# The triangular inverses of the chunk scan: in the scan's matmuls, or ahead on VectorE by forward substitution

## The reference

```python
def step(state, inp):
    r_t, w_t, k_t, v_t, a_t, b_t = inp
    sa = jnp.einsum('bhij,bhj->bhi', state, a_t)
    state = (state * w_t[:, :, None, :] + sa[..., None] * b_t[:, :, None, :]
             + v_t[..., None] * k_t[:, :, None, :])
    return state, jnp.einsum('bhij,bhj->bhi', state, r_t)
```

## Time and profile before

| | us |
|---|---|
| median of 3 runs | 2294.08 (2293.27 to 2294.53) |
| the profiled execution: its time | 2291.64 |
| the profiled execution: its span | 2289.8 |
| PE busy (matmuls) | 2108.6, 92% of the span |
| DVE busy | 732.4, 32% |
| ACT busy | 483.5, 21% |
| POOL busy | 282.9, 12% |
| mean granted clock of PE | 0.967 of full speed |

### The profile page before, as it was taken

How to read it: one execution, slowest core, us unless ns; L and a number is a source line. 1 busy time by engine, 2 the same in 40 slices (tenths; PEclk the granted TensorE clock), 3 DMA queues, 4 the chain that set the end, 5 groups by cost and what they waited for, 6 DMA issues and landing times.

```text
span 2289.8 us, 30661 instructions
## 1 busy us (share of the span) xinstructions
PE 2108.6 (92%) x11820; PEld 1261.8 (55%) x11820; DVE 732.4 (32%) x1860; ACT 483.5 (21%) x1206; POOL 282.9 (12%) x569
## 2 busy tenths in 40 slices
PE   6999999999998799999999599999997999999994
PEld 2343389999983644444444246666646444444441
DVE  4212655555558321111111240346513211111113
ACT  2212244444431100000000110156611000000001
POOL 0000365555530000000000100001100000000001
PEclk9999999999999799999999799999997999999997
DMA  9371000000012679999999461100025799999994
GB/s 267 42 152 64 28 1 2 2 2 1 2 38 98 275 298 416 428 427 430 428 425 430 156 232 54 74 19 23 17 110 220 315 425 430 425 429 430 426 423 156
DMA packets 54453, 493.57 MB, mean 216 GB/s; under 512 B 8740, under 2 KB 13348, under 8 KB 37414
## 3 DMA queue, kind: packets, MB, share of 16 engines
q1 hardware_dynamic: 39670, 461.10, 49.2%
q10 hardware_dynamic: 12336, 22.09, 4.0%
q0 software_dynamic: 2304, 8.39, 1.0%
HBM read 458.46 MB, written 32.05 MB: 214 GB/s over the span
## 4 chain that ended last, share of the span: by engine, by line
PE 89%; DVE 5%; issue 2%; ACT 2%; DMA 1%; POOL 1%; ACTq 0%; DVEq 0%; POOLq 0%
PE bank L1293 85%; PE bank L1800 2%; DVE arena L1096 1%; PE bank L1522 1%; PE bank L1600 1%; DVE arena L1253 1%; PE bank L1301 1%; POOL arena L501 1%; DMA arena<-y_rows,ints 0%; DVE arena L799 0%; DMA arena<-x 0%; PE bank L1465 0%; ACT arena L525 0%; ACT arena L774 0%; DVE arena L1264 0%
## 5 line engine op out<-in xcount | busy, mean ns | idle before, releaser
L1293 PE MATMUL bank<-arena 128*128 128x128 f32 (+8 forms) x10232 | 1933.1, 417 | 69.4 <-DVE arena L1096 44.4
L1293 PEld LDWEIGHTS bank<-arena 128*128 128x128 f32 (+4 forms) x10232 | 1106.0, 173 | 831.3 <-issue 732.8
L643 ACT ACTIVATE arena<-bank 128x256 f32<-128x256 f32 (+3 forms) x512 | 176.6, 351 | 216.5 <-PE bank L1293 158.3
L671 ACT ACTIVATE arena<-bank 128x512 f32<-128x512 f32 x64 | 38.2, 597 | 823.2 <-PE bank L1293 823.2
L501 POOL DMA_INDIRECT arena<-y_rows,ints x16 | 17.9, 1116 | 1218.7 <-DMA y_rows<-arena 1214.5
L432 POOL TENSOR_TENSOR arena<-arena,const 128x128 f32<-128x128 f32 x384 | 147.9, 414 | 111.0 <-PE bank L1293 88.5
L1034 DVE TENSOR_TENSOR arena<-bank,vec 128x512 f32<-128x512 f32 x64 | 44.2, 691 | 346.3 <-PE bank L1293 346.3
L1088 DVE TENSOR_TENSOR arena<-arena,bank 128x256 f32<-128x256 f32 x64 | 26.9, 421 | 339.2 <-ACT arena L667 339.2
L930 DVE TENSOR_TENSOR arena<-bank,arena 128x128 f32<-128x128 f32 x256 | 70.4, 291 | 57.8 <-PE bank L1293 57.4
L774 ACT ACTIVATE arena<-arena,small 128x128 f32<-128x128 f32 (+3 forms) x128 | 70.4, 552 | 25.1 <-DVE small L1253 25.1
L1096 DVE COPY arena<-bank 128x256 f32<-128x256 f32 x64 | 26.9, 420 | 144.7 <-PE bank L1600 144.7
(11 more groups left out here) (198 smaller groups left out, 1077.4 us busy)
## 6 DMA issues: line engine op xcount, KB each, us to landing
arena<-m_w SPq DMA_DIRECT2D x64, 4096.0 KB, 21.0
arena<-m_w SPq DMA_DIRECT2D x64, 2048.0 KB, 13.6
y_rows<-arena ACTq DMA_DIRECT2D x128, 128.0 KB, 9.4
y_rows<-arena SPq DMA_DIRECT2D x2, 3840.0 KB, 41.8
arena<-kv_w SPq DMA_DIRECT2D x3, 2048.0 KB, 12.4
rev_bias<-arena ACTq DMA_DIRECT2D x1, 5120.0 KB, 55.6
arena<-a_wk SPq DMA_DIRECT2D x8, 512.0 KB, 16.1
arena<-a_wv SPq DMA_DIRECT2D x8, 512.0 KB, 3.4
```

What stands on the lines that cost most here:

```text
L643: nc.scalar.activation(dst(n), src, ACT.Copy).then_inc(sem("ev_" + name), 1)
L671: nc.scalar.activation(yb[:, n % 2, :], bank[6 + n % 2][:, :], ACT.Copy).then_inc(sem("yb_ready"), 1)
L1293: return nc.tensor.matmul(dst, lhsT, rhs, start=start, stop=stop)
```

## The change

The triangular inverses are taken out of the scan.

- The v projection comes after k as before, but tile by tile with its own copy of the mix (`mix_v`); its weights are laid out for that. In its second half PE issues `k_inverse` and, for each m, a block of 16 small products `gram_of(m)`, which DVE masks into `gram` (`gram_out`). For this a and b are made complete beside v, no longer beside r.
- SP stores the two 32x32 diagonal blocks of every head and chunk to DRAM, four transfers for each m (`store_gram`), between the loads of the weight ring. When all 32 have landed, it loads them back with the two blocks of one head and chunk on each of the 128 partitions (`solve`).
- DVE then makes the inverses of the two 32x32 blocks on each partition by forward substitution: for column i from 2 to 31 a product of i x i elements (twice) and a sum over one axis, each waiting for the one before (60 operations).
- SP stores the inverses, and loads them back, in 128-byte runs, into the places of the Gram blocks.
- Only then ACT makes the decays again (`tmp` shares its memory with `solve`), DVE the bonus operand and r, POOL the scaled k, and PE the bonus products.
- The scan is a loop of `PACKS + 6` ticks. Its PE order is rh, u, w, u2, y, s, tr. POOL makes the block-diagonal inverse from `gram` (`x_e`), and w and u2 put in the off-diagonal 32x32 part: two products on 32 rows and 32 columns of weights each. The decay of the state moves from POOL to ACT. The results of y go to r's region, and the first four parts of `w_o` are loaded before the scan ends.

The core of the diff, PE's scan and projections, DVE's solve and SP's list:

```diff
+            for m in range(4):
+                store_gram(m)
+            sp.wait_ge(sem("proj_mm"), 13)
+            load_ring(16, d["a_wr"][0, :, :])
+            for m in range(4, NP):
+                store_gram(m)
+            sp.wait_ge(sem("proj_mm"), 14)
+            load_ring(17, d["a_wr"][1, :, :])
+            sp.wait_ge(sem("gram_out"), 32 * 16)
+            sp.wait_ge(sem("a_ready"), NP)
+            sp.wait_ge(sem("b_ready"), NP)
+            sp.dma_start(solve, gram_dram.rearrange("h n b s t -> (h n) b s t")).then_inc(sem("solve_in"), 16)
+            for m in range(2, NP):
+                sp.wait_ge(sem("proj_mm"), 13 + m)
+                load_ring(16 + m, d["a_wr"][m, :, :])
+            sp.wait_ge(sem("solved"), SOLVED)
+            sp.dma_start(inverse_dram.rearrange("h n b s t -> (h n) b s t"), solve).then_inc(sem("inverse_out"), 16)
...
+            def store_gram(m):
+                sp.wait_ge(sem("gram_ev"), m + 1)
+                for hh in range(2):
+                    for b in range(2):
+                        lo = 64 * hh + 32 * b
+                        sp.dma_start(gram_dram[hh, m::NP, b, :, :].rearrange("c s t -> s c t"),
+                                     gram[lo:lo + 32, m::NP, 32 * b:32 * b + 32]).then_inc(sem("gram_out"), 16)
...
+            nc.vector.memset(ones_at, 1.0).then_inc(sem("solved"), 1)
+            for i in range(2, 32):
+                dve.wait_ge(sem("solved"), 2 * i - 3)
+                terms = products[:, 0:2 * i * i].rearrange("p (b c j) -> p b c j", b=2, c=i)
+                nc.vector.tensor_tensor(terms, solve[:, :, 0:i, 0:i], spread(solve[:, :, 0:i, i], 2, i),
+                                        ALU.mult).then_inc(sem("solved"), 1)
+                dve.wait_ge(sem("solved"), 2 * i - 2)
+                nc.vector.tensor_reduce(solve[:, :, 0:i, i], terms, axis=AX.X, op=ALU.add).then_inc(sem("solved"), 1)
...
+            act.wait_ge(sem("inverse_out"), 16)
+            for m in range(NP):
+                if m >= 2:
+                    act.wait_ge(sem("operands_dve"), m - 1)
+                    act.wait_ge(sem("operands_pool"), m - 1)
+                nc.scalar.activation(tmp[:, 1, m % 2, :], l_T[:, m, :], ACT.Exp, scale=-DECAY)
+                nc.scalar.activation(tmp[:, 2, m % 2, :], l_T[:, m, :], ACT.Exp, scale=DECAY).then_inc(sem("decays"), 1)
...
+            def gram_of(m):
...
+                for c in range(T // C):
+                    for lo in (0, 64):
+                        last = mm(bank[6 * (m % 2)][lo:lo + 64, C * c:C * c + C], b_T[lo:lo + 64, m, C * c:C * c + C],
+                                  a_T[lo:lo + 64, m, C * c:C * c + C])
+                last.then_inc(sem("gram_mm"), 1)
...
+                n = tick - 3
+                if 0 <= n < PACKS:
+                    if n in (0, 16):
+                        pe.wait_ge(sem(f"inverse_in{n // 16}"), 64)
+                    pe.wait_ge(sem("ev_u"), n + 1)
+                    if n:
+                        pe.wait_ge(sem("ev_w"), n)
+                    for lo in (0, 64):
+                        last = mm(p_w[lo + 32:lo + 64, :], gram[lo:lo + 32, n, 32:64], u_s[lo:lo + 32, n % 4, lo:lo + 64])
+                    last.then_inc(sem("pe_w"), 1)
```

More of the change, by code:

```diff
@@ L147, in decoder_program @@
         chunk_decay = small[:, 16:80].rearrange("p (m c) -> p m c", m=NP)
+        solve = region(2)[:, 0:2048].rearrange("p (b s t) -> p b s t", b=2, s=32)
+        ones_at = region(2)[:, 0:2048].rearrange("p (b n) -> p b n", b=2)[:, :, 0:1024:33]
+        products = region(2)[:, 2048:4096]
+        gram_dram, inverse_dram = (nc.dram_tensor(name, (2, PACKS, 2, 32, 32), FP32, kind="Internal").ap()
+                                   for name in ("gram", "inverse"))
         stage_at = [2 * U]
@@ L286, in decoder_program @@
         NORM_AT = (0, 1, 2, 6, 7)
+        SOLVED = 1 + 2 * 30
         block = stack.enter_context(nc.Block())
@@ L304, in _ @@
             sp.dma_start(g2r[0:32, :], d["a_g2"][128:160, :]).then_inc(sem("lora2_in"), 16)
[L306 to L322, removed]
+            wk_rows = d["a_wk"].rearrange("(k p) n -> k p n", k=NK)
@@ new lines, in _ @@
+            sp.wait_ge(sem("solved"), SOLVED)
+            sp.dma_start(inverse_dram.rearrange("h n b s t -> (h n) b s t"), solve).then_inc(sem("inverse_out"), 16)
+            sp.wait_ge(sem("inverse_out"), 16)
+            for part, (lo, hi) in enumerate(((0, 16), (16, PACKS))):
+                for hh in range(2):
+                    for b in range(2):
+                        row = 64 * hh + 32 * b
+                        sp.dma_start(gram[row:row + 32, lo:hi, 32 * b:32 * b + 32],
+                                     inverse_dram[hh, lo:hi, b, :, :].rearrange("n s t -> s n t")
+                                     ).then_inc(sem(f"inverse_in{part}"), 16)
@@ L324, in _ @@
+            for m in range(4):
+                sp.wait_ge(sem("proj_mm"), 21 + m)
+                load_ring(24 + m, wo_rows[m, :, :])
             sp.wait_ge(sem("pe_s"), PACKS)
             sp.wait_ge(sem("ev_s"), PACKS)
[L326 to L330, removed]
+            for m in range(4, NP):
+                sp.wait_ge(sem("wo_used"), m - 3)
+                load_ring(24 + m, wo_rows[m, :, :])
@@ L447, in _ @@
             pool.wait_ge(sem("bonus_ev"), NP)
[L448 to L451, removed]
+            for tick in range(-1, PACKS):
                 n = tick + 1
@@ L608, in _ @@
-            act.wait_ge(sem("scan_done"), NP)
+            for m in range(NP):
+                act.wait_ge(sem("proj_mm"), m + 1)
+                nc.scalar.activation(k_T[:, m, :], bank[m][:, :], ACT.Copy).then_inc(sem("proj_ev"), 1)
+            act.wait_ge(sem("proj_ev"), 8)
+            act.wait_ge(sem("cmp_bias"), 16)
+            for m in range(NP):
+                nc.scalar.activation(a_T[:, m, :], k_T[:, m, :], ACT.Square,
+                                     scale=v8("kk")[:, m:m + 1]).then_inc(sem("k_sq"), 1)
@@ new lines, in _ @@
+            pe.wait_ge(sem("gram_ev"), NP)
+            for m in range(NP):
+                pe.wait_ge(sem("rk_ready"), m + 1)
+                if m >= 2:
+                    pe.wait_ge(sem("bonus_ev"), m - 1)
+                mm(bank[6 + m % 2][:, :], head_ones, tmp[:, 3, m % 2, :]).then_inc(sem("bonus_mm"), 1)
+            pe.wait_ge(sem("bonus_ev"), NP)
+            pe.wait_ge(sem("operands_pool"), NP)
+            for tick in range(PACKS + 6):
+                n = tick - 1
+                if 0 <= n < PACKS:
```

536 lines of the change are left out of this document (249 added, 287 removed).

## The result

Before 2294.31 us (median of 4 runs, 2293.27 to 2295.12), changed 2204.46 us (2195.74 to 2207.59, 4 runs): ratio 0.9603, 95% interval 0.9573 to 0.9632. Forecast 2202. The changed kernel scatters over 12 us, the old one over 2 (6.4 at most in the series of the experiments); experiment 2 shows from where. The profiled execution took 2202.11 us with a span of 2200.1.

A forecast was written before the change was run, and what follows sets the result against it. PE was taken to bound the scan. 130 us saved there less 39 lost at its start, with 1 or 2 for smaller effects, gave 92 us; span 2199.6, plus 2.4 to the median: 2202 us, range 2168 to 2250.

The forecast's parts named there:

- What a tick loses and keeps: PE's scan tick of 5.95 us: 3.4 us of removed products go, 2.55 us stay.
- Corners: Scan tick: w and u2, 8 records on 32x32 corners, add 0.6 us (0.46 products, 0.15 switches; bounds 0.2 and 1.0).
- Stall: Scan tick: rh waits for ACT's 384-column copy of the transposed operands and DVE's two masks, 0.8 us per tick.
- Rival 2: Scan: a second wait per tick, such as PE meeting DVE's corner additions, 47 us more, 2249 us; chance 0.10.
- Fill and drain: Scan: five filling ticks about 11 us plus 4 for the half clock, six draining ticks about 10 us.
- Gram products and stores: Beside v: last Gram product at 221.7, stores landed by 227, load of 1 MB done at 231.5.
- rival 1: SP's queue: 32 stores between weight loads at 1.9 us each instead of 0.45, 61 us, r's ring late, 2232; chance 0.08.
- Solve: DVE's 60 dependent operations: products 35.0, sums 21.7, fixed 11.7, together 68.5 us, ending at 300; bounds 55 and 100.
- Rival 3: Solve: price of reading down a column well above the nearest row's, solve 100 us, 2233 us in all; chance 0.08.
- Decays: Before the scan: 2.3 to 2.4 us a tile as DVE and POOL exclude each other; 21.5 us with entry.
- Start: First scan product at 328.2 against 289.2 before, so the start is lost by 39 us.
- rival 4: Scan: PE stays at 1.2 GHz, tick 6.8, 168 us on top, 2370; slower from 32 low ticks; chance 0.06.

The follow-up runs named there:

- experiment 2: Changed kernel plus unread products where PE idled before the scan (18 behind r, one behind each bonus product, two behind the last): 2190.41 us, ratio 0.9556.
- experiment 7: Kernel with transpositions and late products moved up behind rh, with each corner product of w and u2 done twice: 2156.2 us, one run.
- experiment 1: Changed kernel with the entering pack's transpositions and late products put second in PE's tick, ACT's copy and DVE's masks moved up too: 2143.52 us, ratio 0.9343.
- experiment 3: Changed kernel, two edits, one run each: solve's products read row i in line instead of column i, 2208.3 us; solve stopped after column 15, 2207.47 us.
- experiment 6: Changed kernel with POOL's product of k with its decay factor left out: 2250.07 us, one run.
- experiment 4: Changed kernel with DVE copying the solve's next column into a contiguous buffer: alone 2207.64 us; with unread products 2179.87; with transpositions moved up 2128.93.

## Why the prediction was right, step by step

- **What a tick loses and keeps.** 2.55 kept, forecast; 3.86 less 0.78 and 0.33 leaves 2.75. The 0.2 more stands at rh and behind the corners (0.30 and 0.27 to the next start where 0.22 was usual) and in the eight records after those (0.95 where 0.90 was).
- **Corners.** 0.6 forecast, 0.33 measured, inside the bounds (0.2 to 1.0). The composition was wrong: I had 0.46 for the products and 0.15 for switches, experiment 7 gives 0.12 for the products and leaves 0.2.
- **Stall.** 0.8 forecast, 0.78 measured, by the meeting that the earlier trace rows showed; experiment 1 shows that it was the only wait in the tick. Rival 2 (a second wait) fell.
- **Full tick.** 3.95 forecast, 3.86 measured: 5 us less over the scan.
- **Fill and drain.** 11 us of fill forecast, plus 4 for the half clock: experiment 2, at the high level throughout, took 11.6 (249.9 less 59 x 3.86 and a drain of 10.6), the changed kernel 20.9. The low level lasted 24 us, not the 7 of the earlier trace rows, and cost 9. The drain of 10.6 (578.93 to 589.48) was forecast as 10. The scan as a whole, 258 forecast and 259.1 measured, is this near by luck: 5 us too much in the full ticks and 6 too little in the fill cancel.
- **Gram products and stores.** The last block ran from 218.0 to 219.1 (forecast 221.7): a block took 1.1 us where I had 1.9. The last store was issued at 223.2 and had landed at 224.8 (227). The stores lie 0.49 apart in SP's queue where they follow each other, 0.65 and 1.05 with their waits, and nothing was late for it: rival 1 fell. The load behind them took 8.4 us for 1 MB where I had 4.5 (5.3 to 8.5 in all kernels that have it), so the solve started at 233.5 instead of 231.5.
- **Solve.** 68.5 us forecast, 69.4 measured. The last product 3.43 and the last sum 2.16 are the 3.4 and 2.2 of the forecast; 1.68 ns for a column element, from a row that read 16 apart, is 1.70 at 32 apart. Rival 3 fell. Its bound was mis-stated: a column price four times as high makes the solve 108 us, not 100. What the Trainium skill says of 16-byte lines (SBUF — State Buffer, Specifications (TRN2)) agrees with experiment 3, where the last product takes 2.16 in line, and with the equal price at 16 and 32 apart.
- **Decays.** 21.5 us forecast from the landed store, 21.7 measured (306.8 to 328.5). The pitch of 2.40 was right, and so in the main were its parts: 0.6 for L990, 1.1 for POOL, with the mask beside it, and 0.6 for the rest of rk. What experiment 6 adds is that POOL's 1.1 are not saved with it (0.42), since the mask then comes into the line and rk alone has a pitch of 0.77. The rule of the Trainium skill that such operations lock each other out (SBUF — State Buffer, Who interferes with whom) agrees with rk's 1.65 and 1.16 beside POOL, 0.74 without, and with the mask's 0.68, which reads one operand from PSUM.
- **Start.** 328.2 forecast, 330.34 measured: 2.0 from the solve's later start, 0.9 from the solve, 0.3 from decays and expansions, less 1.1 for the store, which took 3.9 where I had 5.
- **The clock, rival 4.** It had 0.06 and a place of its own; the mechanism was real and the size was off. It entered the scan at the low level, as the rival said, and a full low tick costs 2.68 (6.54 less 3.86; forecast 2.85). But it left it after one full tick in the profiled run, and after eight to ten in the profiled runs of the four kernels of experiments 3, 4 and 6 that have the gap and no unread products. The 32 that decide were never near. My sign for a wrong forecast, a clock that swings, came in part: 24 us instead of some 7. My rows against it misled. In 686:696 PE was at the high level already, and staying there is not the same as getting there; from 696 to 706, busy for 3.7 us of ten, it was at 0.67. And in 290:297 it was the old scan that left the low level, whose ticks have no gap (PE busy for 385.4 of 388.4 us).
- Open: why the changed kernel left the low level after 24 us and its four relatives only after 69 to 82. Their idle times before the scan differ in place and length, and I did not vary these alone; chance has a part too, as the four runs of the column copy show (experiment 4).

## What to carry to other kernels

When a change moves PE's idle time to just before a long stage, price the entry of that stage at the low clock, and look at every gap inside its ticks: a shorter way to the start was worth nothing until the gap was gone or filled, or the clock kept up before it. The evacuation of a pack belongs behind other products of the same tick; put what another engine must copy early in PE's order, not last. Where the time of a stage does not answer to an edit that its own rows show to work, read the granted clock before looking for a new wait.

## Of the hardware, not expected

- PE at the low level stayed there for 69 to 82 us of the scan in four profiled runs while busy for nine tenths of the time (50 of 55 us in the one shown), with one idle time of 0.63 us in each full tick of 6.54 us; with the gap filled it left within 5 us of the scan's start, and without the gap within 9 to 12. In one further kernel with the gap, the changed one, it left after 24.
- At the high level the same gap, 0.63 of 3.86 us, did no harm for over 220 us (354 to 579 in the changed kernel, at 1.00).
- Corner products of 32x32, 64 columns: 0.015 us per record among their like, and some 0.2 us once per tick around them.
- POOL's product of 512 elements, 1.7 us long, held up DVE's rk (both inputs in SBUF) until it ended, 0.74 becoming 1.16 or 1.65, and the mask (one input in PSUM) not at all.
- The same 1 MB load, issued between 223.8 and 225.7 us behind 32 stores of short runs, took 5.3 to 8.5 us in thirteen kernels; the solve and with it the scan's start move by as much.
